# Turning the units of the block-wise norm in pairs behind every second chunk of the mixing stage

## The reference

```python
y_attn = block_attention(q, k, v) @ w_attn_branch[l]
y_four = fourier_mix(f) @ w_fourier_branch[l]
y = (g_a * y_attn + g_f * y_four) @ w_out[l]
x = x + gate1 * rms_norm(y, mix_post_g[l])

h = rms_norm(x, ffn_pre_g[l]) * (1.0 + scale2) + shift2
u = depthwise_conv_centred(h @ w_up[l], conv_w[l], conv_b[l])
```

## Time and profile before

| | us |
|---|---|
| median of 3 runs | 3378.85 (3377.94 to 3382.74) |
| profiled execution, its own time | 3376.42 |
| span of the profiled execution | 3374.6 |
| TensorE busy | 3161.7 (94%) |
| VectorE busy | 2431.2 (72%) |
| ScalarE busy | 1244.8 (37%) |
| mean granted TensorE clock | 0.97 |

### The profile page before, as it was taken

One profiled execution on the slowest core, in us unless ns is written; L12 is line 12 of the kernel. 1 busy time (PEld: TensorE's weight loads), 2 busy tenths in 40 slices (PEclk: granted clock), 3 DMA queues, 4 the chain that ended last, 5 costly groups with the idle time before them and its releaser, 6 DMA issues.

```text
span 3374.6 us, 35384 instructions
## 1 busy us (share of the span) xinstructions
PE 3161.7 (94%) x13945; PEld 2544.2 (75%) x13945; DVE 2431.2 (72%) x2669; ACT 1244.8 (37%) x1614; POOL 223.3 (7%) x307
## 2 busy tenths in 40 slices
PE   3789999998799999959999999999999899999997
PEld 3667777776678888847777888888888788888885
DVE  6639787775399999966656467677677667676777
ACT  4113211110599999933343332222223321212222
POOL 2101504432000000000000000000000000000000
PEclk7899999999899999979999999999999999999999
DMA  5643422322612111147675621221225211111113
GB/s 200 215 157 136 160 87 73 106 94 96 218 44 45 35 35 34 33 129 212 215 221 200 221 80 47 61 61 41 61 61 179 91 61 41 61 41 61 41 61 120
DMA packets 137942, 349.33 MB, mean 104 GB/s; under 512 B 27144, under 2 KB 36232, under 8 KB 133288
## 3 DMA queue, kind: packets, MB, share of 16 engines
q1 hardware_dynamic: 120176, 303.02, 28.4%
q10 hardware_dynamic: 12096, 25.17, 2.0%
q0 software_dynamic: 5504, 18.88, 1.5%
HBM read 249.58 MB, written 92.19 MB: 101 GB/s over the span
## 4 chain that ended last, share of the span: by engine, by line
PE 46%; DMA 4%; DVE 4%; ACT 1%; SPq 1%; issue 1%; DVEq 0%; ACTq 0%
PE second_ps_a L90 10%; PE second_ps_a L92 10%; PE second_ps_a L91 10%; PE second_ps_b L90 6%; PE second_ps_b L91 6%; PE second_ps_b L92 6%; DMA merge_w_st<-in_w_branch 2%; DMA merge_st_b<-scratch_rec 1%; DVE second_y L2064 1%; DMA merge_x<-scratch_rec 0%; ACT merge_wb_hi L1590 0%; DVE second_y L2082 0%; DVE second_y L2079 0%; DMA ffn_x<-scratch_x 0%; SPq L1532 0%
## 5 line engine op out<-in xcount | busy, mean ns | idle before, releaser
L2064 DVE TENSOR_TENSOR second_y<-second_y,second_ps_b 128x512 f32<-128x512 f32 x654 | 444.3, 688 | 212.6 <-PE second_ps_b L92 212.6
L90 PE MATMUL second_ps_a<-second_h_hi,up_wu_hi 128*128 128x512 f32 x1408 | 549.6, 390 | 4.3 <-DVE up_wu_lo L1813 4.3
L91 PE MATMUL second_ps_a<-second_h_lo,up_wu_hi 128*128 128x512 f32 x1408 | 549.0, 390 | 0.0
L92 PE MATMUL second_ps_a<-second_h_hi,up_wu_lo 128*128 128x512 f32 x1408 | 549.0, 390 | 0.0
L1204 DVE TENSOR_TENSOR att_prob_lo<-att_prob,att_prob_hi 128x1024 fp32r<-128x1024 f32 x256 | 309.8, 1221 | 26.0 <-ACT att_prob_hi L1170 25.0
L90 PEld LDWEIGHTS second_ps_a<-second_h_hi,up_wu_hi 128*128 128x128 f32 x1408 | 264.9, 188 | 60.4 <-DVE up_wu_lo L1813 5.2
L92 PEld LDWEIGHTS second_ps_a<-second_h_hi,up_wu_lo 128*128 128x128 f32 x1408 | 265.1, 188 | 55.3
L91 PEld LDWEIGHTS second_ps_a<-second_h_lo,up_wu_hi 128*128 128x128 f32 x1408 | 265.1, 188 | 55.1
L90 PE MATMUL proj_ps<-h_hi,proj_w_hi 128*128 128x512 f32 x704 | 293.0, 416 | 9.1 <-DVE proj_w_lo L731 9.1
L90 PE MATMUL second_ps_b<-ffn_wd_hi,ffn_g_hi 128*128 128x512 f32 x704 | 276.6, 393 | 20.9 <-ACT second_y L1982 12.1
L91 PE MATMUL second_ps_b<-ffn_wd_lo,ffn_g_hi 128*128 128x512 f32 x704 | 275.4, 391 | 0.0
(11 more groups left out here) (227 smaller groups left out, 5844.9 us busy)
## 6 DMA issues: line engine op xcount, KB each, us to landing
up_w_st<-in_w_up SPq DMA_DIRECT2D x88, 512.0 KB, 5.9
ffn_wd_st<-in_w_dn SPq DMA_DIRECT2D x44, 512.0 KB, 3.6
fin_ada_w<-in_w_ada SPq DMA_DIRECT2D x32, 512.0 KB, 5.1
scratch_gates<-proj_out SPq DMA_DIRECT2D x64, 256.0 KB, 2.0
merge_w_st<-in_w_branch SPq DMA_DIRECT2D x32, 512.0 KB, 6.4
merge_gate<-scratch_gates SPq DMA_DIRECT2D x64, 256.0 KB, 3.4
scratch_h<-merge_x ACTq DMA_DIRECT2D x48, 256.0 KB, 4.9
proj_w_st<-in_w_z SPq DMA_DIRECT2D x22, 512.0 KB, 4.6
```

The costliest lines, as they stand in the source:

```text
L90: pe.matmul(out, w_hi, x_hi, start=first, stop=False)
L91: pe.matmul(out, w_hi, x_lo, start=False, stop=False)
L92: return pe.matmul(out, w_lo, x_hi, start=False, stop=last)
L2064: dve.tensor_tensor(at, at, ps_d[:, q % 4, :], ALU.add).then_inc(s_y, 1)
```

## The change

One table is written anew. Behind chunk 1 the units 0 and 1 are turned, behind chunk 3 the units 2 and 3, behind chunk 5 the units 4 and 5; chunk 7 keeps units 6 and 7; chunks 2, 4 and 6 have none.

```diff
-    TURNS = {1: [0], 2: [1], 3: [2], 4: [3], 5: [4], 6: [5], 7: [6, 7]}
+    TURNS = {1: [0, 1], 3: [2, 3], 5: [4, 5], 7: [6, 7]}
```

## The result

The changed kernel takes 3400.72 us (median of 6 runs, 3396.88 to 3406.9), the one before on the same chip 3378.53 us (6 runs, 3377.9 to 3386.71). The ratio is 1.0061, with a 95% interval of 1.0047 to 1.0075: about 22 us slower, where 3398 us had been forecast. The profiled execution has a span of 3399.2 us, 24.6 us more than before, with the same instructions.

The account below looks back on a forecast made before the run. TensorE was taken to set the pace, with a loop through weight copies and loads almost level. Terms 12.1 + 0 + 3 + 2 + 3.4 = +20.5 us led to a forecast of 3398 us (+0.6%), range 3386 to 3410.

Parts of the forecast that it names:

- The pair adds 2.93 us to each odd turn: Chunks 1, 3, 5: merged low part ends 6.34 us after merge starts, against 3.41 us with a single unit.
- Room of about 0.3 us for TensorE: Mixing chunks: TensorE needs 11.8 us for two chunks, so it sees loop delays of more than about 0.3 us.
- Both paths: Blocks 1 to 3: late weight copies delay chunks 3, 5, 7, later loads keep pace with TensorE; 12.1 us together.
- Loads, taken as 4.49 us: Weight loads issued in odd chunks land after 4.49 us, no store beside them; term 0, between 0 and 12.8 us.
- Stores, 3 us between 0 and 8.4: Units 3 and 5 wait 0.5 us each for stores from the same buffer, twice a block: 3 us.
- The next block's operands, 2 us: Attention loads issued 1.1 us nearer chunk 7's end, without cover: 2 us for two blocks, between 0 and 2.4.
- The clock, 3.4 us for two stretches: Two of nine new TensorE idle stretches are followed by 1.2 GHz, 1.7 us each: 3.4 us, between 0 and 8.5.
- the signs: Trace signs: three copy waits of about 2 us a block, merge(1) to chunk 7's end 41 to 44 us.
- hidden after all: Rival: second unit slips beside merge and weight copies, only better loads count; about 3375 us, chance 0.04.
- Half of it: Rival: only the load path counts in the blocks, +5 to +11 us, some 3386 us; chance 0.08.
- Stores as in chunk 7: Rival: units 3 and 5 wait 5.6 us at six places for stores, 51 us in all, 3428 us; chance 0.05.

Follow-up runs that it names:

- The kernel before with early loads: The kernel before, with SyncE issuing the next weight load ahead of its wait for the merged low part, in all blocks: 3361.3 us, ratio 0.9962.
- With early loads: The changed kernel, with SyncE issuing the next weight load ahead of its wait for the merged low part, in all blocks: 3377.02 us, ratio 1.0003.
- the kernel with four buffers: The changed kernel, with units 2 and 3 held in two buffers of their own: 3391.51 us, ratio 1.0044.
- the same edit in blocks 1 to 3: The changed kernel, with weight loads issued ahead of SyncE's wait in blocks 1 to 3 only, block 0 as before: 3389.41 us, ratio 1.0048.
- the kernel with copies ahead: The change with loads issued early and, in chunks 1, 3, 5, chunk m + 2's weight split before the units, merged parts before the second: 3369.78 us.

## Why the prediction was right

The direction and the mechanism held, copies and loads that stand behind the pair. The size came out near because errors of both signs met, which is partly luck. Term by term:

- **The pair adds 2.93 us to each odd turn**, the low part of the merged rows 6.34 us after merge: 6.37 us measured. Chunk 3 was to start 7.95 us after merge(1), and starts 1622.68 - 1614.85 = 7.83 us after it.
- **Room of about 0.3 us for TensorE: misread.** The prediction's own numbers have the loop at 12.14 us and TensorE's work at 11.8, so the loop was already the longer one. The kernel before with early loads shows it, with 35.2 us in blocks 2 and 3 for 37.72 (1.7 of them slow clock) and 38.11.
- **Both paths.** The forecast had 12.1 us from the copy and the load path together. With early loads, which leave only the copy path, the blocks are 10 us over before; the other 14 of the 24 us are what the change loses through its loads, with stores and clock. Since early loads give the kernel before 4.9 us in the blocks too (107.2), the copy path costs 15 us against a kernel with the same loads.
- **Loads, taken as 4.49 us (0 between 0 and 12.8): mis-sized.** On the path they took 5.53, 4.72, 4.80 and 5.63 us in the chain's rows, and 4.6 us twice in block 2. The stores had moved away as forecast: that of unit 0 in block 1 is issued at 1617.49 us and the next at 1627.73, and the load of 5.53 us lies between the two. It still took a microsecond more than the one of 4.49 us. The mean of the six is 5.0 us, six times 0.5 us more: some 3 us.
- **Stores, 3 us between 0 and 8.4: 5.6 us.** The landings in the chain, 6.04, 6.80, 7.17 and 5.72 us, lie in the range that was read from the earlier trace rows. That row was called undisturbed, but a weight load was issued 0.06 us behind the store, and the stores that units 3 and 5 wait for have such a neighbour, too. In block 1 the load for chunk 5, issued at 1626.81 us, took 6.5 us beside the store of unit 1. The store of unit 2, issued at 1632.58, has no such load beside it but for its first 0.8 us. From issue to landing, the two halves of the store of unit 1 and then those of unit 2:

```profile
DMA to landing us min/median/max: 4.2/5.1/6.0
```
```profile
DMA to landing us min/median/max: 2.2/2.5/2.7
```

  The rule of the Trainium skill that was weighed there (DMA: Bandwidth & Descriptors, section Anatomy of one DMA) gives an estimate of 3.2 us for such a store. The trace agrees for the store of unit 2, 3.1 us from the first issue to the second landing, and not for the stores on the path. These decide, and the kernel with four buffers shows that most of what they seem to cost is on the path.
- **The next block's operands, 2 us: none.** The stretch between blocks is 0.13 and 0.44 us shorter, and TensorE waits 0.42 us for the fourth tile in block 1, 0.20 before. This step failed. In block 1 the four loads are issued 1.2 us nearer to chunk 7's end, as forecast, but the last of them lands 14.8 us after the first issue and not 17.3 as before, so against chunk 7's end it lands 1.2 us earlier. In block 2 they are not issued nearer to it at all.
- **The clock, 3.4 us for two stretches:** there are four, and all four count against the forecast, since its 12.1 us already takes off the slow stretch of block 2 before: 6.8 us. Three of them follow waits that a store had lengthened, 2.58, 3.93 and 3.75 us, beyond the 2.0 to 2.2 us forecast (0.7, 2.1 and 1.85 us of them by the reading above), so this term was not independent of the stores.

So loads, stores and clock were together taken 9.0 us too low and the operands 2 too high, which makes 27.5 us out of 20.5. The blocks lost 24.0. Some 3.5 us of these terms lay under something else. The forecast had merge(3) at 14.0 us after merge(1) but TensorE free only at 14.45; merge(3) came at 15.1, and of the 1.1 us only 0.65 moved chunk 4. And the slow stretch of block 3 ran while the load of 5.63 us was on its way: the split of chunk 6's weights began at 1851.80, which with 2.23 us puts merge(5) at 1854.03 at the earliest, and it started at 1854.15. Only these two covers were read off; the rest is not shown.

Of the signs, the pairs of transposes, the waits ahead of chunks 3, 5 and 7 (1.70 to 3.93 us) and the slow stretches came. Two others were missed: from merge(1) to the end of chunk 7 the blocks take 44.9, 46.6 and 45.1 us and not 41 to 44, and ScalarE waits 3.4 us in the first pair for VectorE, not 2.

The rivals: "hidden after all" fell with the first wait. "Half of it", the load path alone, seemed to come true with early loads, and was refuted by the same edit in blocks 1 to 3. "Stores as in chunk 7" did not happen with the change; a store wait of 4.0 us did arise at unit 3, but only in the kernel with copies ahead, where the store it waits for is issued behind merge(3).

## What to carry to other kernels

Work that is off the critical path still sets a period when it stands in an in-order queue ahead of something that closes a loop: in chunks 2 to 7 the same units cost 24 us or nothing, depending on what was queued behind them and on their buffers. Follow the loop round all engines (copy, merge, low part, load issue, landing) and compare it with the bound engine's own work for the same turn; a loop level with it has no room for batching. Look, too, for a wait on the issuing engine that a transfer doesn't need: passing it (the load ahead of the wait) gave the kernel before 16 us. And price a wait for a buffer by the landing beside the transfers that will really run then: from the first issue to the last landing, a unit's store took 3.1 us nearly alone and 6.1 to 7.8 us beside a weight load, on the path of the change. When an edit that should undo a cost brings the total back exactly, look stretch by stretch before believing it: the gain may come from a place that never had the cost.

## What was not expected of the hardware

The stretches of slow clock don't follow the length of one wait. In the kernel before with early loads, three waits of 1.76 us ahead of chunk 2 were followed by one stretch at 0.50 (block 1), two not. With early loads under the change, waits of 2.05, 1.96 and 2.13 us were followed by none, where the earlier trace rows have one behind 2.07 us and the change one behind 1.89 us. I can't say from these runs what decides.

The 512 KB weight loads on the path of the changed kernel took from 4.7 to 5.6 us to land, although no store was issued within the first 4.8 us of any of the four in the chain, and the store before each had landed. Before, 4.49 us without a store and 5.56 to 6.62 us beside one had looked like two cases. What else sets it was not tried.
